# A two-layer encoder on one core: constants of the next layer prepared in the last product, and some turned tiles in other groups

## What is computed

```python
x = layer_norm(x, ln0)
for i in range(2):
    qa, ka, va, qb, kb, vb = split(x @ w_in[i])             # widths 512,128,128,512,128,128
    oa = attention(rope2d(rms(qa) * q_norm[i]), rope2d(rms(ka) * k_norm[i]), va)   # 8 heads, softmax over 256
    ob = window_sink_attention(rope1d(qb), rope1d(kb), vb, sink[i])                # 8 heads, band of 128
    x = layer_norm(ALPHA * x + concat(rms(oa), rms(ob)) @ w_out[i], ln1[i])
    g, v = split(x @ w_up[i])                               # 2 x 2816
    ffn = (gelu(conv3(g, conv_w[i], conv_b[i])) * v) @ w_down[i]
    gate = sigmoid(x @ w_ple_gate[i] + b_ple_gate[i])
    x = layer_norm(ALPHA * x + ffn + gate * (p[i] @ w_ple[i]), ln2[i])
```

## Time and profile before

| | us |
|---|---|
| runs (3) | 1215.14, 1215.49, 1216.63; median 1215.49 |
| the profiled execution | 1215.36 |
| its span | 1213.6 |
| PE busy | 1192.3 (98%) |
| POOL, DVE, ACT busy | 593.9, 526.7, 492.4 |
| mean granted clock of PE | 0.997 |
| the layer's edge | about 612 |

### The profile page before, as it was taken

How to read it: one execution, slowest core, us unless ns; L and a number is a source line. 1 busy time by engine, 2 the same in 40 slices (tenths; PEclk the granted TensorE clock), 3 DMA queues, 4 the chain that set the end, 5 groups by cost and what they waited for, 6 DMA issues and landing times.

```text
span 1213.6 us, 17810 instructions
## 1 busy us (share of the span) xinstructions
PE 1192.3 (98%) x5800; PEld 974.2 (80%) x5800; DVE 526.7 (43%) x1098; ACT 492.4 (41%) x899; POOL 593.9 (49%) x342
## 2 busy tenths in 40 slices
PE   7999999999999999999999999999999999999997
PEld 6887778888888888888878777788888888888886
DVE  7777847532122134211477777375211122431108
ACT  3456753344344333323144767433443333332321
POOL 6665844455443444344155756634653444434442
PEclk9999999999999999999999999999999999999999
DMA  6321213344333332222132202433433333222331
GB/s 220 88 74 49 88 45 113 113 130 139 98 92 87 103 104 95 79 97 95 56 90 70 80 27 70 126 116 89 139 104 104 100 90 102 90 85 91 102 104 70
DMA packets 122854, 115.68 MB, mean 95 GB/s; under 512 B 6816, under 2 KB 97952, under 8 KB 122784
## 3 DMA queue, kind: packets, MB, share of 16 engines
q1 hardware_dynamic: 122784, 114.81, 30.7%
HBM read 112.70 MB, written 2.10 MB: 95 GB/s over the span
## 4 chain that ended last, share of the span: by engine, by line
PE 93%; DVE 2%; DVEq 1%; issue 1%; POOL 1%; DMA 1%; ACT 0%; SPq 0%; ACTq 0%
PE ps L1219 28%; PE ps L1221 28%; PE ps L1220 28%; PE ps L1371 3%; PE ps L1385 3%; PE ps L1359 1%; PE ps L1361 1%; PE ps L1342 1%; PE ps L1229 1%; POOL w_lo L537 1%; DMA scratch<-in_ln_b_dram 1%; DVEq L875 0%; DVEq L1202 0%; DVE x L880 0%; POOL ln_r L533 0%
## 5 line engine op out<-in xcount | busy, mean ns | idle before, releaser
L527 POOL TENSOR_TENSOR w_lo<-raw,w_hi 128x1024 fp32r<-128x1024 f32 x192 | 461.7, 2406 | 411.4 <-ACT w_hi L635 411.4
L1219 PE MATMUL ps<-xt_hi,w_hi 128*128 128x512 f32 x704 | 273.9, 389 | 0.0
L1220 PE MATMUL ps<-xt_lo,w_hi 128*128 128x512 f32 x704 | 273.9, 389 | 0.0
L1221 PE MATMUL ps<-xt_hi,w_lo 128*128 128x512 f32 x704 | 273.9, 389 | 0.0
L635 ACT ACTIVATE w_hi<-raw 128x1024 fp32r<-128x1024 f32 x192 | 201.9, 1055 | 132.7 <-PE ps L1221 66.6
L1219 PE MATMUL ps<-w_hi,stat 128*128 128x512 f32 x480 | 188.3, 392 | 0.0
L1220 PE MATMUL ps<-w_lo,stat 128*128 128x512 f32 x480 | 187.1, 390 | 0.0
L1221 PE MATMUL ps<-w_hi,stat 128*128 128x512 f32 x480 | 187.0, 390 | 0.0
L1219 PEld LDWEIGHTS ps<-xt_hi,w_hi 128*128 128x128 f32 x704 | 132.1, 188 | 27.6
L1220 PEld LDWEIGHTS ps<-xt_lo,w_hi 128*128 128x128 f32 x704 | 132.1, 188 | 27.5
L1221 PEld LDWEIGHTS ps<-xt_hi,w_lo 128*128 128x128 f32 x704 | 132.1, 188 | 27.3
(11 more groups left out here) (123 smaller groups left out, 1330.8 us busy)
## 6 DMA issues: line engine op xcount, KB each, us to landing
raw<-in_w_up_dram SPq DMA_DIRECT2D x88, 512.0 KB, 3.8
raw<-in_w_down_dram SPq DMA_DIRECT2D x44, 512.0 KB, 3.2
raw<-in_w_in_dram SPq DMA_DIRECT2D x26, 512.0 KB, 3.8
raw<-in_w_out_dram SPq DMA_DIRECT2D x16, 512.0 KB, 3.8
raw<-in_w_ple_gate_dram SPq DMA_DIRECT2D x16, 512.0 KB, 3.9
scratch<-in_ln_g_dram SPq DMA_DIRECT2D x5, 512.0 KB, 4.5
scratch<-in_ln_b_dram SPq DMA_DIRECT2D x5, 512.0 KB, 6.0
raw<-in_w_ple_dram SPq DMA_DIRECT2D x4, 512.0 KB, 3.7
```

The source lines that it names most:

```text
L527: pool.tensor_tensor(w_lo[:, n, :], raw[:, n % RAW, :], w_hi[:, n, :].bitcast(F32), ALU.subtract).then_inc(w_split.sem, 1)
L1219: pe.matmul(out, a[0], b[0], start=first, stop=False)
L1220: pe.matmul(out, a[0], b[1], start=False, stop=False)
L1221: return pe.matmul(out, a[1], b[0], start=False, stop=last)
```

## The change

- PE's order: ("rot", 2, t) stands in groups 7, 11, 15, 19 instead of 6, 10, 14, 18; the second half of the side input is turned in group 27 instead of 26. ACT's and DVE's halves of them move by the same one group.
- DVE: mean_squares of groups 15, 23, 31 stands right behind maxima instead of late in the group.
- SP: the constants of layer 0 are loaded ahead of the loop; those of the next layer (in the second layer: those of layer 0 once more) after the looped loads of the last product, behind a wait for the last gated tile. A wait for them is added at the end.
- DVE: the tables are made ahead of the loop, and in the loop before the norms of the last product.
- DVE: norm_lo(1) stands behind the last tile's norm and its drain, as the last thing in the loop.

```diff
-        if g in (6, 10, 14, 18):
-            steps.append(("rot", 2, (g - 6) // 4))
-        if g in (25, 26):
-            steps.append(("p_t", g - 25))
+        if g in (7, 11, 15, 19):
+            steps.append(("rot", 2, (g - 7) // 4))
+        if g in (25, 27):
+            steps.append(("p_t", (g - 25) // 2))
...
+            def load_constants(layer):
+                sp.dma_start(cols[:, :], columns[bass.ds(layer, 1)].rearrange("a p n -> (a p) n")).then_inc(const_landed.sem, 16)
...
+            load_constants(0)
             with sp.Fori(0, DEPTH) as layer:
...
-                sp.wait_ge(h_done.sem, h_done.at(layer, 0))
...
                         load(s, down_source(layer, i * 2 + v), 1)
+                following = (layer + 1) % DEPTH
+                sp.wait_ge(h_done.sem, h_done.at(layer, FT))
+                load_constants(following)
                 for r in range(1, REST):
                     raw_free(DOWN_AT + LOOPED + r)
...
+            sp.wait_ge(const_landed.sem, const_landed.at(DEPTH, 64))
...
-                    if g in (7, 11, 15, 19):
-                        qkt_evac(2, (g - 7) // 4)
+                    if g in (8, 12, 16, 20):
+                        qkt_evac(2, (g - 8) // 4)
...
-                    if g in (26, 27):
-                        k = g - 26
+                    if g in (26, 28):
+                        k = (g - 26) // 2
...
             dve.wait_ge(fixed_landed.sem, 16)
+            gain_tables(64)
             with dve.Fori(0, DEPTH) as layer:
...
-                dve.wait_ge(const_landed.sem, const_landed.at(layer, 64))
-                for i in range(2):
...
                 norm_lo(2, xt_hi_done.at(layer, 1))
...
-                    if g in (7, 11, 15, 19):
-                        qkt_lo(2, (g - 7) // 4)
+                    if g in (15, 23, 31):
+                        mean_squares((g - 15) // 8)
+                    if g in (8, 12, 16, 20):
+                        qkt_lo(2, (g - 8) // 4)
...
-                    if g in (15, 23, 31):
-                        mean_squares((g - 15) // 8)
...
+                gain_tables(const_landed.at(layer, 128))
                 for t in range(TT - 1):
                     wait_down(dve, layer, t)
                     norm_sum(t, DOWN_BANK[t], ln_rstd.at(layer, 4 + t + 1), norm_landed.at(layer, 64), down_free)
-                    if t in (1, 2):
-                        norm_lo(t - 1, xt_hi_done.at(layer, 13 + 2 * (t - 1)))
+                    if t == 1:
+                        norm_lo(0, xt_hi_done.at(layer, 13))
...
                 dve.drain().then_inc(down_free.sem, 1)
+                norm_lo(1, xt_hi_done.at(layer, 15))
```

More of the change, by code:

```diff
@@ L431, in _ @@
             sp.dma_start(rope_sb[:, :, :, :], rope).then_inc(fixed_landed.sem, 16)
-            with sp.Fori(0, DEPTH) as layer:
-                def raw_free(s):
-                    sp.wait_ge(w_split.sem, w_split.at(layer, s - AHEAD - RAW + 1))
-                sp.wait_ge(h_done.sem, h_done.at(layer, 0))
+            def load_constants(layer):
                 sp.dma_start(cols[:, :], columns[bass.ds(layer, 1)].rearrange("a p n -> (a p) n")).then_inc(const_landed.sem, 16)
@@ L442, in _, with raw_free @@
                 sp.dma_start(sinks[:, :], bcast(sink[bass.ds(layer, 1)].rearrange("a n -> (a n)"))).then_inc(const_landed.sem, 16)
+            load_constants(0)
+            with sp.Fori(0, DEPTH) as layer:
+                def raw_free(s):
+                    sp.wait_ge(w_split.sem, w_split.at(layer, s - AHEAD - RAW + 1))
                 for s in range(AHEAD, UP_AT):
@@ L484, in _ @@
                     load(DOWN_AT + LOOPED + r, down_source(layer, LOOPED + r), 1)
-                following = (layer + 1) % DEPTH
                 for s in range(AHEAD):
@@ L909, in _, with gain_tables @@
                     norm_lo(t - 1, 2 * t - 1)
+            def gain_tables(landed):
+                dve.wait_ge(const_landed.sem, landed)
+                for i in range(2):
+                    g = gains[:, i, :].unsqueeze(1).to_broadcast([P, 2, HD])
+                    gs = (gains[:, i, :].rearrange("p (i b) -> p i b", b=2)[:, :, ::-1].unsqueeze(1)
+                          .to_broadcast([P, 2, HD // 2, 2]))
+                    dve.tensor_tensor(rope_a[:, 2 * i, :, :], rope_sb[:, 0, :, :], g, ALU.mult)
+                    dve.tensor_tensor(rope_a[:, 2 * i + 1, :, :].rearrange("p t (i b) -> p t i b", b=2),
+                                      rope_sb[:, 1, :, :].rearrange("p t (i b) -> p t i b", b=2), gs, ALU.mult)
+                dve.tensor_scalar(neg_sinks[:, :], sinks[:, :], -1.0, None, ALU.mult)
+                dve.drain()
+                dve.tensor_scalar(rope_a[:, 2:4, :, :], rope_a[:, 2:4, :, :], 8.0, None, ALU.mult)
+                dve.drain()
             dve.wait_ge(fixed_landed.sem, 16)
+            gain_tables(64)
             with dve.Fori(0, DEPTH) as layer:
```

## The result

| us | before | after |
|---|---|---|
| median | 1216.06 (1215.14 to 1216.82, 4 runs) | 1206.53 (1205.78 to 1207.04, 4 runs) |
| the profiled execution | 1215.36 | 1206.90 |
| its span | 1213.6 | 1205.1 |

The ratio of the times is 0.992, with a 95% interval of 0.9909 to 0.9932. In five more runs the changed kernel had a median of 1206.46 (ratio 0.9924, 0.991 to 0.9937). Predicted were 1207.3 and "faster". From profile to profile 8.46 us went, where the sum said 8.02; from median to median it is 9.5.

The account below looks back on a forecast made before the run. TensorE, busy 98% of the span, was taken as the bound, so only its standing time could be won. Groups 5.26, end 0.85 and edge 1.91 sum to 8.02 us: 1215.36 to 1207.3, range 1205.5 to 1211.2.

Parts of the forecast that it names:

- Groups 14 and 15: Attention groups: moved tile no longer follows the sum of squares, 0.51 us, and probs_t(12) stops idling, 0.45; 0.96 a layer.
- the yardstick: PE in the attention groups: one turned tile follows another 0.43 us later, start to start, when nothing is late.
- Side input: Groups 25 and 26: second half turned one group later no longer waits for the first's bank; 1.67 us a layer.
- What is queued behind: Moved low halves, 1.28 us on DVE, delay later maxima and exponentials; 0.6 us of cover left, so no new waits.
- Constants: Early loads cost nothing on SP; tables made in DVE's idle 16.10 us cost nothing, 1.5 us if that cover were gone.
- The jump: Layer's edge: norm_lo(1) runs within DVE's 2.81 us jump back, so norm_lo(2) begins near 620.4 instead of 622.46.
- A: Layer's edge: the jump doesn't hide norm_lo(1), whose 1.29 us stand ahead of it; 1208.6 us, chance 0.12.
- The edge: Between layers: rotated tile ready 2.06 us earlier, PE's third product starts at 625.25 instead of 627.16; 1.91 us.
- theory F: Made after the result: DVE's program arrives in pieces; past the jump, DVE stands at a fixed program place until the next arrives.
- The end: Kernel's end: with norm_lo(1) behind the last tile, the second half-sum starts and the last tile finishes 0.85 us earlier.
- C: Attention groups: moved low halves make scores wait at all eight places, so slower; up to 1227.8 us, chance 0.03.
- D: Groups 14 to 28: DVE and ACT pace them, stalls return as waits for exp, only 2.76 us remain; 1212.6, chance 0.07.

Follow-up runs that it names:

- the lengthened kernel: The changed kernel with four 128x128 multiplications, each with a drain, on VectorE ahead of each of the four moved lower halves: 1221.03 us.
- the first experiment: The changed kernel with norm_lo(1) back ahead of the last tile: 1207.75 us.

## Why the prediction was right, and where not

- **Groups 14 and 15**: 0.96 predicted, 1.00 measured. Putting the tiles back cost 0.52 there, for 0.51 in the step. The distance behind a probs_t was 0.50, not the 0.43 of the yardstick. The 0.45 for oss I had put down to both edits together; each alone removes it, so the moved mean_squares adds next to nothing to the moved tiles.
- **Side input**: 1.67 predicted, 1.79 measured. Undone alone it costs 4.09 us in layer 0 and 2.45 in layer 1.
- **Lesser gaps**: in the groups up to 14 and from 16 to 25 another 0.48 us went in layer 0 and 0.41 in layer 1, which stood in the prediction only as 0.8 us for the low end. This is the largest part of what the sum lacked.
- **What is queued behind**: "the cover is thin" was right, and "0.6 us is left" was on the wrong chain. I followed the exponentials; the nearest wait is that of probs_t for the bank that the low half reads, with 0.68, 0.29 and 0 us at the first three places; the third is the worked one. That no new wait appeared was in part luck: the term "none" rested on 0.6 us of cover where the lengthened kernel found none.
- **Constants**: no wait for a raw load in the last product, no cost on SP's side. The tables run in DVE's idle time, as said, but not in 1.5 us: they stand from 570.27 to 576.03, for two of their multiplications run beside POOL's subtractions and take 2.50 and 2.48 us instead of 0.28. DVE is idle for another 10.42 us behind them, so nothing of it shows in the time; but without that cover they would cost up to 5.8 us at this place, not the 1.5 that the prediction names.

```profile
570.67 2.50 DVE L923 TENSOR_TENSOR rope_a<-rope_sb,late 128x128 f32<-128x128 f32 x1
```

```profile
570.54 4.89 POOL L533 TENSOR_TENSOR w_lo<-raw,w_hi 128x1024 fp32r<-128x1024 f32 x2 [3.04 <-ACT w_hi L641]
```

- **The jump**: right to 0.03 us; A is refuted by the rows at 613.58 and 616.91 and by the first experiment. **PE's loss** for the banks that norm_lo(1) reads: 0.45 predicted, all of it at the second bank. Measured 0.39 + 1.00 us from 613.94 to 615.33, where 617.45 to 618.47 had taken 1.02 before: 0.37, of it 0.16 ahead of the first bank and 0.21 behind.
- **The edge, the term that failed**: 1.91 predicted, 0.95 measured in the profile of the result. The failing step is "norm_lo(2) begins near 620.4 ... and the rotated tile is ready 2.06 us earlier". The first half holds. The second took the time from norm_lo(2) to the rotated tile over from the kernel before, with a pause of 0.46 us inside it that I hadn't looked at. That pause is tied to a place in the program (a fetch, by theory F) and measured from 0.46 to 2.33 us. In the execution where it was 0.81, the edge gave 1.85.
- **The end**: 0.85 predicted and measured.
- **C and D** fall: no wait for an exponential appears, and the groups gave all they promised. That the total is right is partly luck: it came out near because 1.3 us too little in the groups (0.69 and 0.62 in the two layers) stood against 1.0 too much at the edge.

**Open**: what sets the size of the second pause. It was 0.46 in three variants and in the kernel before, 0.81 and 1.57 in two executions of the changed kernel, and 1.09, 1.13 and 1.39 in three others. The share of DMA around it doesn't sort them: in the two stretches of 2 us around it DMA was busy 0.42 and 0.55 with the pause of 1.57, and 0.43 and 0.56 with one of 0.46 (mean_squares late).

## What to carry to other kernels

When a trace has "issue" for the releaser inside work that you mean to move closer to a jump, take it as a possible fetch with a size of its own, not as part of the work's duration, and shift the program by a few idle instructions to see whether it moves; queued work without a drain behind it runs under the jump. Where two turned things share two banks, a whole group between them is worth more than an earlier reader, and a stand that is read off as 1.7 us can come to 4 once the engine runs further ahead and its clock falls. A cover is best measured by inserting work until something waits: that also names the chain which is the next to be late.

## What the runs showed of the hardware that I had not expected

- DVE's second pause behind a jump: tied to the place in the program, and 0.46 to 2.33 us long. Far from a jump such a pause was 0.29 to 0.43 us long.
- In the lengthened kernel one inserted multiplication of 128x128 in each layer, both operands in SBUF, took 2326 ns where the median of the 32 is 293. POOL's subtraction of a weight slice, 2.45 us long, had begun at 134.23, between the first and the last of the four; the same stands at 729.88 beside the long one of layer 1 (729.54, 3.67 us). Beside the six short insertions POOL was idle. The Trainium skill, "SBUF — State Buffer", section "SBUF: two separate sides", says that such a DVE instruction and a POOL instruction that reads SBUF lock each other out of a shared pair of ports for a whole instruction; these rows agree, and so do the 2.50 and 2.48 us of the tables beside POOL in the changed kernel, where the same multiplications took 0.28 to 0.29 us in the variant that makes them at the head of the loop, with POOL idle. So that experiment charged its fourth place with more than was meant.
- PE's granted clock was 0.52 for about 3 us behind a stand of 2.17 us in layer 0, and 1.00 behind a stand of the same 2.17 us in layer 1, with the same work around both. In the lengthened kernel it stayed at 1.00 behind a stand of 1.85 us in layer 0 and fell to 0.50 behind the same stand in layer 1. What makes the difference was not tried.
